# In the first recurrence, TensorE works the second chunk of a round one product behind the first

## The reference, cut to what matters

```
def step(S, inp):
    r_t, d_t, k_t, v_t, kk_t, b_t = inp
    sk = jnp.einsum('bhvk,bhk->bhv', S, kk_t)
    S = S * d_t[:, :, None, :] - sk[..., None] * b_t[:, :, None, :] + v_t[..., None] * k_t[:, :, None, :]
    return S, jnp.einsum('bhvk,bhk->bhv', S, r_t)
```

## Time and profile before

| | us |
|---|---|
| time, median of 3 runs | 4489.44 |
| the 3 runs | 4482.98 to 4498.09 |
| profiled execution: its span, first to last instruction | 4487.2 |
| from the first `mx` to the first `rhs` | 763.68 to 786.01 |
| rounds 0 to 6 of the state part, by the first `mt` of each | 786.95 to 1078.54 |

### The profile page before, as it was taken

One profiled execution on the slowest core, in us unless ns is written; L12 is line 12 of the kernel. 1 busy time (PEld: TensorE's weight loads), 2 busy tenths in 40 slices (PEclk: granted clock), 3 DMA queues, 4 the chain that ended last, 5 costly groups with the idle time before them and its releaser, 6 DMA issues. The chain is left out here.

```text
span 4487.2 us, 85729 instructions
## 1 busy us (share of the span) xinstructions
PE 4217.4 (94%) x32575; PEld 3820.4 (85%) x32575; DVE 3222.2 (72%) x6008; ACT 1430.6 (32%) x2183; POOL 1565.4 (35%) x1316
## 2 busy tenths in 40 slices
PE   7999998999677989999999998999999999999997
PEld 4888887878555878978888887999999999999996
DVE  5631334555845237899985665999999999999997
ACT  2211322111634222233336665222222222222223
POOL 6433333564031210044443323444343443434430
PEclk9999999999858999999999999999999999999998
DMA  4655665455542320134434455999999999999994
GB/s 170 206 188 190 205 229 195 178 194 183 146 130 89 127 82 34 43 123 146 142 127 174 172 202 200 336 300 301 299 302 302 299 302 298 303 301 298 303 299 153
DMA packets 523006, 928.01 MB, mean 207 GB/s; under 512 B 284032, under 2 KB 351232, under 8 KB 518688
## 3 DMA queue, kind: packets, MB, share of 16 engines
q1 hardware_dynamic: 387024, 549.29, 37.1%
q0 software_dynamic: 80960, 346.96, 22.6%
q10 hardware_dynamic: 54816, 28.85, 2.2%
HBM read 785.79 MB, written 206.30 MB: 221 GB/s over the span
## 5 line engine op out<-in xcount | busy, mean ns | idle before, releaser
L3285 POOL DMA_INDIRECT ex_rows<-expert_rows,ex_here x512 | 583.2, 1139 | 955.6 <-DVE acc_tok L3420 852.7
L3420 DVE SCALAR_TENSOR_TENSOR acc_tok<-ex_rows,ex_wsp,acc_tok 128x1024 f32<-128x1024 f32 x512 | 633.7, 1278 | 0.2 <-issue 0.2
L2652 PE MATMUL ex_psa<-x_dense_high,eg_u_high 128*128 128x288 f32 x2048 | 605.1, 295 | 11.1 <-ACT ex_w L3348 8.0
L2743 POOL TENSOR_TENSOR eg_u_low<-eg_u,eg_u_high 128x1024 fp32r<-128x1024 f32 x130 | 330.4, 2542 | 803.8 <-ACT eg_u_high L2738 803.8
L2652 PE MATMUL ex_psa<-x_dense_low,eg_u_high 128*128 128x288 f32 x2048 | 604.9, 295 | 0.0
L2652 PE MATMUL ex_psa<-x_dense_high,eg_u_low 128*128 128x288 f32 x2048 | 604.6, 295 | 0.0
L3317 PE MATMUL ex_pso<-ex_w_high,ex_v_high 128*128 128x288 f32 x2048 | 441.0, 297 | 9.7 <-DVE acc L3402 9.5
L3348 ACT ACTIVATE ex_w<-ex_psa 128x288 f32<-128x288 f32 x256 | 105.2, 411 | 1054.0 <-PE ex_psa L2652 1033.5
L3317 PE MATMUL ex_pso<-ex_w_high,ex_v_low 128*128 128x288 f32 x2048 | 439.7, 296 | 0.0
L3317 PE MATMUL ex_pso<-ex_w_low,ex_v_high 128*128 128x288 f32 x2048 | 438.2, 296 | 0.0
L3402 DVE TENSOR_TENSOR acc<-ex_pso,acc 128x576 f32<-128x576 f32 x512 | 373.7, 750 | 47.0 <-PE ex_pso L3317 47.0
(11 more groups left out here) (514 smaller groups left out, 9547.4 us busy)
## 6 DMA issues: line engine op xcount, KB each, us to landing
eg_u<-in_u SPq DMA_DIRECT2D x256, 512.0 KB, 3.3
expert_rows<-in_v SPq DMA_DIRECT2D x128, 512.0 KB, 6.9
ex_v<-in_v SPq DMA_DIRECT2D x128, 512.0 KB
weights<-wt_stage SPq DMA_DIRECT2D x9, 4096.0 KB, 13.1
ex_g<-weights SPq DMA_DIRECT2D x128, 288.0 KB
expert_rows<-eg_act SPq DMA_DIRECT2D x256, 128.0 KB, 1.7
proj<-in_out POOLq DMA_DIRECT2D x50, 548.5 KB, 6.1
in_w<-in_w_in SPq DMA_DIRECT2D x50, 512.0 KB, 4.7
```

Of the source, the lines that this page charges most:

```text
L2652: yield nc.tensor.matmul(out[:, 0:b - a], w[:, kc, :], half[:, kc, a:b], start=n == 0, stop=n == len(passes) - 1)
L2743: self.k.nc.gpsimd.tensor_tensor(self.ul[par][:, :, :], self.u[par % 2][:, :, :], self.uh[par][:, :, :].bitcast(F32), ALU.subtract).then_i ...
L3285: pool.indirect_dma_start(rows[i][:, :], None, table, index(here[par][:, t, j:j + 1]), element_offset=ROW_RUNS[t][0]).then_inc(s_row[i], 16)
L3420: v.scalar_tensor_tensor(out=acc_tok[:, t, :], in0=rows[i][:, at:at + D], scalar=wsp[:, i:i + 1], in1=acc_tok[:, t, :], op0=ALU.mult, op1= ...
```

## The change: what it does

Chunk 1's generator on TensorE has one more `yield` after its first part. From then on it is one turn behind: while chunk 0 does `xmx` of a level, chunk 1 does `mx` of the same level, and while chunk 0 does `mx`, chunk 1 does `xmx` of the level before. A round gets a turn 11, in which chunk 1 does its last `xmx` alone. `staggered_steps` writes the list of step names in that order for TensorE. The code that builds VectorE's and ScalarE's lists is untouched, and every wait stays at its step. The number of instructions is the same.

```
+def staggered_steps(chunks, first, per_level, levels):
+
+    turns = [[None] * h + [f"{s}{lv}_{h}" for lv in range(1, levels) for piece in per_level for s in piece] for h in chunks]
+    turns = [t + [None] * (max(len(u) for u in turns) - len(t)) for t in turns]
+    return [f"{s}_{h}" for h in chunks for s in first] + [s for turn in zip(*turns) for s in turn if s]
@@ rw_matrix_pe
     mm.then_inc(*PE.inc(f"tok_{h}"))
     yield
+    if h:
+        yield
     for lv in range(1, levels):
@@ RwBuffers.__init__
-        self.PE = Progress(k.sem(f"{tag}_pe"), *in_turn_steps(chunks, ["mt", "m", "tok"], [["mx"], ["xmx"]], levels), *each(after_pe))
+        self.PE = Progress(k.sem(f"{tag}_pe"), *staggered_steps(chunks, ["mt", "m", "tok"], [["mx"], ["xmx"]], levels), *each(after_pe))
```

## The result

The changed kernel takes 4509.38 us (median of 6 runs, 4506.92 to 4514.59), the kernel before beside it 4478.89 us. The ratio is 1.0071, with a 95% interval of 1.0054 to 1.0088: about 32 us slower. The forecast was +23 us, reckoned from the 4489 us of the first three runs of the kernel before: 4512, the range 4499 to 4522.

A forecast was written before the change was run, and what follows sets the result against it. TensorE, busy 92% of the rounds, was taken as close to the bound there, a three-engine chain in the first matrix part. +24.6 - 2 + 0.4 = +23 us on 4487.2, plus 2.2, gave 4512; range 4499 to 4522.

The forecast's parts named there:

- Turn 6: In each of seven rounds, u_1 waits 2.26 us for VectorE's copy of rhs_1, queued behind level 2's t and xy.
- Turns 10 and 11: At each round's end, mx5_1 waits 1.35 us for xy4_1, then xmx5_1 waits 0.64 us after mx5_1.
- Turn 5: In each round, mx3_0 waits 0.36 us: 2.74 needed, 2.38 covered by xmx2_1, mx2_1 and rhs_1.
- What goes: The old waits of mx_1 in the rounds disappear: 0.83 us a round by the list, taken as 1.1.
- The sum of the rounds: New waits 4.61 less 1.1 gone, +3.5 us a round, +24.6 in seven; -2 for swallowed issue pauses.
- rival C: In each round the clock falls once more: 1.6 us a round, +11 on top of the forecast, 4523; chance 0.09.
- The first matrix part: Before the rounds: a level still takes 4.65 us, chunk 1's tail takes back the head start; 22.7 against 22.33, +0.4.
- Rival B: TensorE's issue pauses in the rounds are caught up during the new waits: +11 us, 4500; chance 0.14.
- Rival D: Waits of mx_1 go and no new wait matches them, VectorE answering under 2 us: up to -12, 4477 to 4484; chance 0.05.
- Rival E: Nothing to be seen: new waits fall into existing pauses, or something later than TensorE ends the phase; 4489; chance 0.04.
- The lower bound: About +15 us: 2.9 a round if 1.5 goes, xy is shortest and a quarter of the pauses is swallowed.

The follow-up runs named there:

- tail experiment: The changed kernel with turn 9 as s_1, xmx4_1, turn_1, mx5_0, mx5_1, turn 10 as xmx5_0, xmx5_1, and no turn 11: ratio 1.0045 to the kernel before.

## Why the prediction was right

The direction, the place and the mechanism of the waits held, and the time lay in the range. Part of that was luck: the range stood on the 4489 us of the first three runs, and reckoned from the 4479 of six the forecast would be 4502 and the range 4489 to 4512, with the measured 4509 close below its end. The step of +27 to +32 lies at the upper bound of the forecast's own +15 to +31. Step by step:

- **Turn 6**, 2.26 us forecast, 2.14 a round in the list, some 0.2 more if reckoned from starts as the forecast was, and removed by an experiment that touches only VectorE's order.
- **Turns 10 and 11**, 1.35 and 0.64 forecast. Turn 10 waited 0.51 to 1.20 us, 1.06 in the mean of the list (7.4 / 7), turn 11 0.48 to 0.49; with the 0.16 for starts that is 1.22 and 0.65. The tail experiment took most of it away.
- **Turn 5**, 0.36 forecast. Of the eleven waits of `mx` for `xy` in the list, seven are those of turn 10, 7.4 us together, and four of turn 5, 0.23 to 0.40 us each, 1.3 together. In three rounds it was not there: seven times 0.36, 2.5 us, was about twice what came.
- **What goes**: the waits of mx_1, 0.83 by the list, went as forecast: the `mx` waits for `xy` that are left are those of turns 5 and 10.
- **The sum of the rounds**, +22.6 forecast (24.6 - 2). TensorE's idle time grew by 21.7 us in the means of two and three profiles. This is the term that I had reckoned, and it is right within 1 us, which is better than its parts and so partly luck.
- **What was missing**: the clock, which I had put into rival C with a chance of 0.09 and at nothing in the forecast. The new wait of u_1 did bring stretches at 1.2 GHz. Busy time grew by 6.4 us in the means for the same matmuls. By an estimate some 2 us of that are no slower matmuls: the lists of the changed kernel have 12 more pauses in the mean, and at each the last matmul shows 0.16 us or more that would otherwise be overlapped. Rival C had 1.6 us a round, 11 in all; about half came. How much of it lengthened the rounds isn't shown: the kernel before took 4.8 us more busy time in one profile without getting longer. The one price that stands by itself is the first `rhs` block, where TensorE waits for nothing: 0.94 us in three profiles of the kernel before, 1.71 and 1.64 in the two of the changed kernel. With the same tail ahead of it the kernel that is behind in the first part only had 0.93 at the full clock, so this price doesn't come each time.
- **The first matrix part**, +0.4 forecast. The two profiles of the changed kernel have 23.68 and 23.15 us, the three of the kernel before 22.17 in the mean: +1.5 and +1.0. The circle was right, 4.58 to 4.73 us a level. The first level was not: the walk took 0.79 us for its `xy`, and that operation took 1.12 us in the changed kernel and 1.38 in the kernel that is behind there only; in the kernel before it had taken 1.25. Chunk 0's head start shrank by that. Ahead of it ScalarE was busy with the copy of `tok` when mx1_0 was done, and xmx1_0 started 1.39 us after mx1_0 and not 1.16.
- **Rival B** (pauses swallow it): "issue" pauses were 14.2, 12.2 and 13.1 us before, 13.6 and 11.3 after. Of the 2 us that the forecast took off for this, 0.7 came in the means, less than the profiles of one kernel differ by. **Rival D** needed VectorE's answer in under 2 us; it took 2.99 to u_1. **Rival E** fell with the result.
- **The lower bound** of the forecast: its own terms, 7 x 2.9 less a quarter of 14 us of pauses and +0.4, come to about +17, not +15.

The forecast came out 4 to 9 us below the measured +27 to +32. In the profiles' means the rounds grew by 28.2 us, 5.6 more than the 22.6 forecast, the first matrix part by 1.2, 0.8 more, and the first `rhs` block by 0.7, which the forecast didn't have. The 5.6 are of the size of the growth in busy time; how much of that the clock caused stays open.

## What to carry to other kernels

Where two chains share three engines in strict order, shifting them against each other on one engine alone makes new waits: here TensorE's list was shifted, VectorE's was not, and an operation that was ready (the copy) stood behind one that no longer was. With VectorE's copy moved and the tail reordered the loss was gone, but no run of this case gained. Before shifting, add up for every dependent pair how much other work lies between its members; in a loop whose bound is a circle over engines, a shift exchanged the roles in the circle and left its length (4.65 us before, 4.58 to 4.73 after), and the chain that is behind must catch up somewhere, where its waits lie bare unless other work is put there. A wait can cost beyond its own length: after three to five of u_1's seven waits, by profile, the clock fell to 1.2 GHz. In a stage where TensorE is busy for 92%, waits of 0.8 us a round were all that this order could win, and the price of the bad one was 4.0 us a round in the means.

## What the runs showed of the hardware that was not expected

An fp32 matmul of the program is two MATMUL records in the trace (8 heads, "x16"). Matmuls put into a wait are not free of side effects: with 647 more TensorE instructions in seven rounds, the pauses called "issue" grew from 13.6 to 23.6 us. Waits of 1.8 to 2.7 us once a round went with seven or eight stretches at 1.2 GHz in four profiles of the rounds, against one to five in the six profiles without them and without fillers; waits of 0.6 to 0.9 us at nearly every step of the first matrix part went with a granted clock of 1.00. And TensorE's busy time for the same 6585 to 6588 matmuls varied by 4.8 us between two profiles of one unchanged kernel while the stretch kept its length within 0.2 us.
